# Expert outputs of a mixture-of-experts stage: row sums gathered and added on VectorE and stored plainly, instead of an adding scatter; experts taken in an order that alternates their groups

## The reference

```python
p_group = jax.nn.softmax(hf @ w_group, axis=-1)
g_sel = jnp.argmax(p_group, axis=-1)          # one group for each token
le = logits_e[token, g_sel]                   # the 8 experts of that group
top_v, top_i = lax.top_k(le, 2)               # two experts, both of the group
gate = g_w[:, None] * jax.nn.softmax(top_v, axis=-1)
...
y = (jax.nn.silu(xb @ w_gate[e]) * (xb @ w_up[e])) @ w_down[e]
out = segment_sum(y * row_w, row_tok)         # x + out is the result
```

## Time and profile before

| what | value |
|---|---|
| median of 3 runs | 1223.68 us (1217.13 to 1223.85) |
| the profiled execution's own time | 1217.27 us |
| its span, first to last instruction | 1215.5 us |
| PE busy | 1111.2 us, 91% of the span |
| DVE, ACT, POOL busy | 438.8, 328.7, 168.2 us |
| moved by DMA | 297.60 MB in 84831 packets |

### The profile page before, as it was taken

How to read it: one execution, slowest core, us unless ns; L and a number is a source line. 1 busy time by engine, 2 the same in 40 slices (tenths; PEclk the granted TensorE clock), 3 DMA queues, 4 the chain that set the end, 5 groups by cost and what they waited for, 6 DMA issues and landing times.

```text
span 1215.5 us, 26688 instructions
## 1 busy us (share of the span) xinstructions
PE 1111.2 (91%) x11558; PEld 802.1 (66%) x11558; DVE 438.8 (36%) x803; ACT 328.7 (27%) x642; POOL 168.2 (14%) x149
## 2 busy tenths in 40 slices
PE   3998899999997987999949999999999998989995
PEld 3998899976664534889846666666666655655563
DVE  3424564348674532335452212222222212212121
ACT  4422232146574542222211111111111111111111
POOL 0000110299200000000010111111111111111110
PEclk9999898999898997999959999999999999999998
DMA  5326786000105441945588999999999999999983
GB/s 192 120 71 182 213 252 203 1 12 2 36 1 173 139 174 70 297 173 228 193 348 332 380 367 380 371 385 367 373 376 375 372 368 379 382 380 372 373 325 57
DMA packets 84831, 297.60 MB, mean 245 GB/s; under 512 B 11393, under 2 KB 42817, under 8 KB 59095
## 3 DMA queue, kind: packets, MB, share of 16 engines
q1 hardware_dynamic: 77543, 274.48, 61.1%
q0 software_dynamic: 7168, 21.37, 7.7%
HBM read 272.98 MB, written 43.66 MB: 260 GB/s over the span
## 4 chain that ended last, share of the span: by engine, by line
PE 73%; DMA 15%; DVE 4%; SPq 3%; ACT 3%; issue 2%; POOL 0%; ACTq 0%; POOLq 0%; DVEq 0%
DMA w_ring<-in_w_up 11%; PE bank L1987 9%; PE bank L2227 8%; PE bank L2371 8%; PE bank L2375 7%; PE bank L2379 6%; PE bank L2039 4%; PE bank L2405 4%; PE bank L2409 4%; PE bank L2204 3%; PE bank L2168 3%; PE bank L2413 3%; PE bank L2077 3%; PE bank L2350 2%; DMA out_k_all<-kn 2%
## 5 line engine op out<-in xcount | busy, mean ns | idle before, releaser
L2371 PE MATMUL bank<-w_ring,xeT 128*32 128x256 f32 x1536 | 347.1, 383 | 0.0
L2375 PE MATMUL bank<-w_ring,xeT 128*32 128x512 f32 x1536 | 269.7, 600 | 14.7 <-DMA w_ring<-in_w_up 14.0
L2371 PEld LDWEIGHTS bank<-w_ring,xeT 128*32 128x32 f32 x1536 | 166.9, 111 | 55.3 <-issue 2.0
L2405 PE MATMUL bank<-w_ring,hT 128*32 128x256 f32 x768 | 171.7, 380 | 0.0
L2379 PE MATMUL bank<-w_ring,xeT 128*32 128x256 f32 x1536 | 157.9, 382 | 0.0
L1873 DVE SCALAR_TENSOR_TENSOR hid<-sgl,gtab,bank 96x256 f32<-96x256 f32 x32 | 21.9, 685 | 356.3 <-ACT sgl L1433 356.3
L2409 PE MATMUL bank<-w_ring,hT 128*32 128x512 f32 x768 | 133.2, 595 | 1.6 <-ACT hT L1439 1.6
L1987 PE MATMUL bank<-w_hi,xh 128*128 128x256 f32 (+1 forms) x432 | 125.4, 290 | 2.5 <-DVE xl L1495 2.4
L1987 PE MATMUL bank<-w_lo,xh 128*128 128x256 f32 (+1 forms) x432 | 122.3, 283 | 0.0
L1987 PE MATMUL bank<-w_hi,xl 128*128 128x256 f32 (+1 forms) x432 | 122.2, 283 | 0.0
L1622 DVE TENSOR_TENSOR_SCAN keep<-keep,unseen 128x1024 f32<-128x1024 f32 (+7 forms) x64 | 87.8, 1404 | 69.1 <-ACT keep L1233 69.1
(11 more groups left out here) (259 smaller groups left out, 1645.1 us busy)
## 6 DMA issues: line engine op xcount, KB each, us to landing
w_ring<-in_w_gate SPq DMA_DIRECT2D x64, 1024.0 KB, 32.3
w_ring<-in_w_up SPq DMA_DIRECT2D x64, 1024.0 KB, 30.6
w_ring<-in_w_down SPq DMA_DIRECT2D x64, 1024.0 KB, 32.1
w_raw<-in_w_in SPq DMA_DIRECT2D x8, 1024.0 KB, 6.9
k_scr<-in_cache_k SPq DMA_DIRECT2D x32, 256.0 KB, 3.6
v_scr<-in_cache_v SPq DMA_DIRECT2D x32, 256.0 KB, 3.3
pgk<-k_scr SPq DMA_DIRECT2D x32, 256.0 KB, 4.1
pgv<-v_scr SPq DMA_DIRECT2D x4, 1024.0 KB, 6.0
```

Source lines behind the costliest of these rows:

```text
L2371: return pe.matmul(up_right_ps(i, g), xeT[i][:, k, rows_of(g)], w[1][:, k, FA:F], start=first and g != 1, stop=ends, skip_group_check=True)
L2375: pe.matmul(gate_ps(i)[rows_of(g), :], xeT[i][:, k, rows_of(g)], w[0][:, k, :], start=first, stop=ends, skip_group_check=True)
L2405: return pe.matmul(y_right_ps(g), hT[:, ft, rows_of(g)], w[:, ft, DA:D], start=first and g != 1, stop=ends, skip_group_check=True)
```

## The change

- `scatter` is a plain indirect store: no addition in the DMA, empty slots left out (bounds T - 1, as in `gather`). `y_all` and `n_scr` lose their spare rows, and the two transfers that filled these with zeros (L928, L929) go.
- A new indirect DMA, `gather_sums(b)`, gathers the rows' sums so far from `y_all` into `yo[b % 2]`, before block b's product is added to it. GpSimd sets both `yo` to zero at first, since empty slots stay unwritten.
- `add_rows` on VectorE takes the place of `left_rows` on ScalarE and `right_rows` on VectorE: five additions, PSUM plus `yo` into `yo` (96 x 512, 96 x 256, three of 32 x 256), after a wait for the gathered sums. TensorE's `down_product` waits for it alone.
- On GpSimd the order for each block is now: gather_sums(b + 1) once scatter b - 1 has landed, scatter(b), gather(b + 4). Gather and scatter no longer end in a wait of their own (`moved` is gone).
- Block b is expert 8 (b mod 4) + b // 4 instead of expert b, so that two neighbouring blocks belong to different groups and share no token; gather_sums(b + 1) can then be issued before scatter(b).
- Two small tables (`cmp`, `past`) move to another place in SBUF, because `yo` is in use earlier.

```diff
+    def expert_of(b):
+
+        return EPG * (b % NGRP) + b // NGRP
...
-            sp.wait_ge(s_zr, 2)
-            sp.dma_start(n_scr[T:NY, :], zrow[:, :]).then_inc(s_yst, 16)
-            sp.dma_start(y_all[T:NY, :], zrow[:, :]).then_inc(s_yst, 16)
...
-            pool.memset(zrow[:, :], 0.0).then_inc(s_zr, 1)
-            pool.wait_ge(s_zr, 2)
+            for i in range(2):
+                pool.memset(yo[i][:, :], 0.0).then_inc(s_zr, 1)
...
-            def scatter(b):
-
-                pool.wait_ge(s_ya, b + 1)
-                pool.wait_ge(s_yd, b + 1)
+            def gather_sums(b):
+
+                i = b % 2
+                pool.wait_ge(s_sc, 16 * (b - 1)) if b >= 2 else pool.wait_ge(s_zr, 3)
                 if b >= NE:
                     pool.wait_ge(s_sx2, b - NE + 1)
+                pool.indirect_dma_start(out=yo[i][:, :], out_offset=None, in_=y_all,
+                                        in_offset=bass.IndirectOffsetOnAxis(ap=rows_named(b, sidx), axis=0),
+                                        bounds_check=T - 1, oob_is_err=False).then_inc(s_ga[i], 16)
+
+            def scatter(b):
+
+                pool.wait_ge(s_yd, b + 1)
                 pool.indirect_dma_start(out=y_all,
                                         out_offset=bass.IndirectOffsetOnAxis(ap=rows_named(b, sidx), axis=0),
-                                        in_=yo[b % 2][:, :], in_offset=None, compute_op=ALU.add,
-                                        bounds_check=NY - 1).then_inc(s_sc, 16)
-
-            def moved(b):
-
-                if b < NE - 3 or b >= NE:
-                    pool.wait_ge(s_gl[(b + 3) % 2], 16 * ((b + 3) // 2 + 1))
-                pool.wait_ge(s_sc, 16 * (b + 1))
+                                        in_=yo[b % 2][:, :], in_offset=None,
+                                        bounds_check=T - 1, oob_is_err=False).then_inc(s_sc, 16)
...
-            for b in range(3):
+            for b in range(2):
                 gather(b)
+            gather_sums(0)
+            for b in range(2, 4):
+                gather(b)
 
             for b in range(NE - 1):
-                if b + 3 < NE:
-                    gather(b + 3)
+                gather_sums(b + 1)
                 scatter(b)
-                moved(b)
+                if b + 4 < NE:
+                    gather(b + 4)
...
-            def left_rows(b, i):
-
-                act.wait_ge(s_dp, 8 * b + 8)
-
-                since(act, s_sc, 16 * b - 16)
-                act.activation(yo[i][:, 0:512], y_left_ps, ACT.Copy)
-                for g in range(2):
-                    last = act.activation(yo[i][rows_of(g), DA:D], y_right_ps(g), ACT.Copy)
-                last.then_inc(s_ya, 1)
...
-            def right_rows(b, i):
+            def add_rows(b, i):
                 dve.wait_ge(s_dp, 8 * b + 8)
-
-                since(dve, s_sc, 16 * b - 16)
-                dve.tensor_copy(yo[i][:, 512:DA], y_mid_ps)
-                dve.tensor_copy(yo[i][rows_of(2), DA:D], y_right_ps(2)).then_inc(s_yd, 1)
+                dve.wait_ge(s_ga[i], 16 * (b // 2 + 1) if type(b) is int else 8 * (b - i) + 16)
+                dve.tensor_tensor(yo[i][:, 0:512], y_left_ps, yo[i][:, 0:512], ALU.add)
+                dve.tensor_tensor(yo[i][:, 512:DA], y_mid_ps, yo[i][:, 512:DA], ALU.add)
+                for g in range(LANES):
+                    rows = rows_of(g)
+                    last = dve.tensor_tensor(yo[i][rows, DA:D], y_right_ps(g), yo[i][rows, DA:D], ALU.add)
+                last.then_inc(s_yd, 1)
...
             def down_product(b, i):
                 w = weights_of(b, i, 2)
                 pe.wait_ge(s_hl, b + 1)
-                since(pe, s_ya, b)
                 since(pe, s_yd, b)
```

More of the change, by code:

```diff
@@ L62 @@
 OVMAX = -(-T // CAP) - 1
-NY = T + CAP
 NCONST = 3
@@ L524, in hybrid_step @@
     s_tbl = sem("router_tables_ready")
-    s_zr = sem("zero_rows_ready")
+    s_zr = sem("zero_logits_and_rows_ready")
     s_ssq2 = sem("sumsq2_ready")
@@ L547, in hybrid_step @@
     s_gc = sem("block_gates_ready")
-    s_sx2 = sem("scatter_rows_named")
+    s_sx2 = sem("sum_rows_named")
+    s_ga = [sem(f"sums_gathered{i}") for i in range(2)]
     s_gl = [sem(f"gathered{i}") for i in range(2)]
@@ L558, in hybrid_step @@
     s_dp = sem("down_product")
-    s_ya = sem("left_rows_copied")
-    s_yd = sem("right_rows_copied")
+    s_yd = sem("rows_added")
     s_sc = sem("block_scattered")
@@ L672, in hybrid_step, with column_of @@
     OVER = ((6, 7, 8), (2, 3, 5))
+    def expert_of(b):
+        return EPG * (b % NGRP) + b // NGRP
+    def column_of(b):
+        return expert_of(b) if b < NE else b
     assert not {parts.index((NE - 1, j)) % NWS for j in range(3)} & set(OVER[0])
@@ L948, in _ @@
                 load_part(q)
-            sp.wait_ge(s_yst, 16 * (NT + 2))
+            sp.wait_ge(s_yst, 16 * NT)
             sp.wait_ge(s_lgp, NT)
@@ L1079, in rows_named @@
             def rows_named(b, further):
-                return (tab[:, b:b + 1] if b < NE else further[b % 2][:, 0:1]).bitcast(U32)
+                return (tab[:, column_of(b):column_of(b) + 1] if b < NE else further[b % 2][:, 0:1]).bitcast(U32)
             def gather(b):
@@ L1128, in _ @@
                     pool.wait_ge(s_gl[(NE + i) % 2], 16 * ((NE + i) // 2 + 1))
-                pool.wait_ge(s_sc, 16 * NE)
                 for o in range(OVB):
                     with pool.If(n_over > o):
+                        pool.wait_ge(s_sc, 16 * (NE + o))
+                        gather_sums(NE + o)
                         gather(NE + o + 3)
                         scatter(NE + o)
-                        moved(NE + o)
+                        pool.wait_ge(s_gl[(NE + o + 3) % 2], 16 * ((NE + o + 3) // 2 + 1))
+                        pool.wait_ge(s_sc, 16 * (NE + o + 1))
         @block.scalar
@@ L1459, in block_act @@
                 block_left(b + 2, i)
-                left_rows(b, i)
             def last_act(b):
@@ L1465, in last_act @@
                     silu(b + 1, 1)
-                left_rows(b, b % 2)
             def resume_act():
@@ L1858, in hidden @@
                 if type(b) is int:
-                    gates = gtab[:, b:b + 1]
+                    gates = gtab[:, column_of(b):column_of(b) + 1]
                 else:
@@ L1898, in block_dve @@
                 block_right(b + 2, i)
-                right_rows(b, i)
+                add_rows(b, i)
             def last_dve(b):
@@ L1903, in last_dve @@
                     hidden(b + 1, 1)
-                right_rows(b, b % 2)
+                add_rows(b, b % 2)
             def resume_dve():
@@ L2463, in _ @@
             blocks(pe, first_pe, block_pe, last_pe, resume_pe, further_pe)
-_OUTS = {"y_all": (NY, D), "k_all": (T, AW), "v_all": (T, AW), "pool_p": (HIST, PW), "pool_s": (DB, HIST, PW)}
+_OUTS = {"y_all": (T, D), "k_all": (T, AW), "v_all": (T, AW), "pool_p": (HIST, PW), "pool_s": (DB, HIST, PW)}
 _LAYERED = ("cache_k", "cache_v", "state_pool", "w_in", "w_pool", "w_out", "w_group", "w_expert", "w_gate", "w_up",
```

15 lines of the change are left out of this document (7 added, 8 removed).

## The result

The changed kernel takes 1248.90 us (median of four runs, 1246.64 to 1256.80), the one before 1220.95 beside it: 28 us more, a ratio of 1.024, 95% interval 1.020 to 1.029. Forecast were 1235, +11 on the kernel before. The sign and the bound (the weight stream pays) hold; the size is two and a half times the forecast. The profile is of the slowest of the four runs, 1256.8 us with a span of 1255.0, so some 8 us of it are no part of what is to be explained; the profile of before lies 3.7 us under its own median.

What follows compares the result with a forecast made beforehand. The prediction took the weight stream to set the end, although TensorE is busy nearly all the time. Stream +11.5 us and tail -0.6 gave about +11 on the 1223.7 us median, 1235, range 1208 to 1252.

Steps and rivals of the forecast that it cites:

- The adding scatter goes: -1.93: Weight stream, each block: removing the 96-row adding scatter gives back 1.93 us.
- The gather of the sums comes: Weight stream, each block: the new gather costs 1.70 us, priced like the existing gather of block rows.
- The sentence on the ports: DMA into SBUF: partition decides which of 16 ports is used; 128-partition transfers keep each engine on its own port.
- The plain scatter comes: Weight stream, each block: a plain scatter costs only its bytes, 67 rows, 0.64 us.
- theory 2: Follow-up theory on GpSimd's transfers: the DMA engine with most rows sets the price; spreading saves 0.8 us a block.
- The sum for a block: Weight stream: -1.93 + 1.70 + 0.64 = +0.41 us a block, +11.5 us over 28 blocks.
- VectorE and the new wait: VectorE's additions, 2.37 us a block, stay hidden in steady state; the gathered sums arrive with 12 us to spare.
- Rival C: GpSimd's new wait: landings taking twice as long make the sums late; 1250 us and more, chance 0.03.
- The tail, -0.6 us: Kernel's end: +0.4 and +1.0 from later additions, -0.2 and about -1.8 from the plain last scatter.
- A: Weight stream: packets alone count, the gather of sums does not slow weights; faster, 1209 us, chance 0.18.
- B: Weight stream: plain scatter rows cost as adding ones, 1.35 us; +1.12 us a block, 1254 us, chance 0.12.
- D: Weight stream: gather of sums at about 1.3 us, no change, 1224 us, chance 0.10.

Runs made afterwards that it cites:

- e1: Changed kernel without the gathers of sums, VectorE adding onto whatever lies in yo: 1203.18 us, ratio 0.988 to the kernel before.
- e6: Kernel before, its adding scatter leaving out empty slots and each expert's rows spread over the slots: 1201.55 us, ratio 0.985.
- e7: Kernel before, its adding scatter leaving out empty slots and its gather of rows over 128 slots: 1202.43 us, ratio 0.987.
- e2: Changed kernel with the sums gathered from n_scr instead of y_all: 1253.23 us, ratio 1.029 to the kernel before.
- e8: Changed kernel, but gather b+4 waits until scatter b has landed: 1254.61 us, ratio 1.031 to the kernel before.
- e5: Changed kernel with each expert's rows spread over the slots: 1225.46 us, ratio 1.006 to the kernel before.
- e9: Changed kernel with both gathers, block rows and sums, over 128 slots: 1216.14 us, ratio 0.999 to the kernel before.
- e4: Kernel before, with its adding scatter leaving out empty slots and nothing else changed: 1219.61 us, ratio 1.002.

## Why the prediction was right and wrong, step by step

- **The bound.** Right. The weight stream sets the end in both kernels, and whatever frees it (e1, e6, e7) stops at TensorE's floor, at 1201.6 to 1203.2 us; the forecast's floor was 17.9 us under the profile of before, 1199.4.
- **"The adding scatter goes: -1.93."** Right as a window, but it hid a rule. With 96 rows in 96 slots bytes and fullest engine give the same, so the scatters of the kernel before could not tell them apart.
- **"The gather of the sums comes", 1.70 us.** Right in kind, a little low: 1.86 by e1, the upper end of the forecast's 1.58 to 1.9. The forecast saw that its two prices explain 95% of the loss; the rest, 0.19 us, belonged to the gather. e2 shows that it is priced like any gather. The sentence on the ports pointed the right way: it spoke against the change, and the 128-slot form takes about 0.6 us off such a gather.
- **"The plain scatter comes", 0.64 us. This is the step that failed**, the term mis-sized: it measured 0.9 to 1.05 us by e1 and 1.15 in e8's windows. "So a plain store costs its bytes: 67 rows" counted the mean engine. The packets themselves are as cheap as said: in e1 q0 has 9.0% of 460 us of 16 engines, 41.4 us, of which 26 gathers at 0.91 take 23.7; 0.66 us are left for each scatter, 0.157 a row and engine. Six rows of these, as theory 2 puts on the fullest engine, are 0.94 us, an estimate that fits what was measured. The earlier trace rows could not warn of it: those stores had full tiles.
- **The sum for a block**: +0.85 instead of +0.41, over 28 blocks +24 instead of +11.5. The scatter's 0.3 to 0.4 us are the larger part of the miss, the sums' 0.16 the smaller.
- **The first wait** came "some blocks earlier": at 13 instead of 20. **"The waits in all 11 us longer"**: 20 us.
- **VectorE and the new wait.** Right: 2.38 us for the additions, hidden; the sums land 9.0 us after issue, the median; no addition waits for them. Rival C did not happen.
- **The tail, -0.6 us: wrong, it is +5.** Products 30 and 31 end 9.61 us apart instead of 7.45, and the span ends 13.8 us after product 31 instead of 10.6. The windows from 1228 us of the kernel after show the first part (PE, PEld, DVE, ACT, POOL busy, then the granted clock):

```profile
1228.00:1232.00 4.00, 3.96 (x54) 2.39 (x45) 2.25 (x4) 0.01 (x1) 0.00 (x0) 1.00 0.23 61
1232.00:1234.00 2.00, 0.00 (x0) 0.01 (x1) 1.88 (x5) 0.48 (x1) 0.00 (x0) 1.00 0.00 0
1234.00:1238.00 4.00, 3.98 (x32) 2.30 (x36) 0.00 (x0) 0.00 (x0) 0.94 (x1) 0.57 0.24 68
1238.00:1242.00 4.00, 3.09 (x48) 1.79 (x39) 0.81 (x2) 0.00 (x0) 0.00 (x0) 1.00 0.02 4
```

TensorE stands for 2.06 us while add_rows(30) runs (before, 1.56 us for the copy of hT), 0.5 us longer, where 0.4 was forecast. Then the granted clock is 0.57 for 4 us: most of them at 1.2 GHz, which costs 4 x 0.43 = 1.7 us. After the 1.56 us the clock stayed at 1.00. But the pause alone does not decide it. e1, e5 and e9 have the same fall (0.60 or 0.61 in the 4 us behind the pause), while e2 and e8 pause for as long, 2.07 us in e2, and stay at full clock; their products 30 and 31 end 7.93 us apart. e2, the first 4 us behind its pause:

```profile
1231.30:1235.30 4.00, 4.00 (x61) 2.73 (x57) 0.00 (x0) 0.00 (x0) 0.94 (x1) 1.00 0.24 68
```

So 1.7 of the 5 us come in some kernels and not in others that differ only elsewhere, and why is open. The second part: the last rows come 1.0 us later, as forecast, but from the start of the last scatter's instruction to the end there are 10.6 us, against 8.4 before. The last scatter itself did become shorter, as forecast: it lands 3.6 us after its start instead of 5.5. What grew is what follows. SyncE's last wait, after the landing, in the kernel after and in the one before (us in total, times, longest):

```profile
SPq L723 <- PEq L723: 6.8, 1, 6.8
...
SPq L716 <- PEq L716: 2.6, 1, 2.6
```

It is 4.2 us in e1, which has the plain scatter but no gather of sums. From the start of the last scatter to the end there are 10.6 us in e5 and e9 too, and 8.0 in e1. So 4.2 us more stand behind the last landing, and part of it came with the third indirect transfer of each block. Why is open.

- **The rivals.** A was wrong, and for a reason worth keeping: the bytes of a transfer are not its price. Nor did the rule that an adding row counts twice decide it: the adding rows are as dear as it says (0.33 us against 0.157), and the gain from plain ones, 1.93 to about 1.0 us, is still seven tenths of what the bytes give; and the gather of the sums slows the weights, which A leaves out. B came out in size, 1254 against 1248.9, by luck: its 1.35 us are too high by as much as the forecast's 0.64 was too low, and its tail of -0.6 made up for it. Nor is its reason the one: single rows are cheap, 0.157 us of an engine. D did not happen.

+24 us from the stream and +5 in the tail are 29; measured are 28. In the two profiled executions, which lie 7.9 us over and 3.7 under their medians, the spans differ by 39.5 us: 4.0 before product 0, 25.3 up to product 28, 4.8 up to product 30 and 5.4 behind it.

## What to carry to other kernels

Do not price an indirect transfer beside a saturated stream by its bytes alone; the engine with most rows gave the better estimate here. Spread the rows over the slots, and only then skip the empties (together -18 us here, skipping alone 0). Give a gather into SBUF the same number of partitions as the loads it runs beside, even if the extra slots are empty (-0.6 us a gather here). And read the price of a transfer over a long stretch that ends before the stream does, in every kernel that is compared: windows at the start of this stage read 0.99 us where the mean was 1.68, and a stretch that ran past the stream's end made one gather 0.3 us too cheap.

## What the runs showed of the hardware

- Leaving out 29 of 96 rows of a scatter changed the time by nothing (e4, 1.002, 0.999 to 1.004); the same rows spread over the slots were worth 18 us more (e6).
- 32 empty slots added to a gather made it cheaper: 1.63 to 0.83 us beside the weights in one window, 1.80 to 1.00 on the mean of 24 and 25 (e4, e7).
- A skipped slot of an indirect transfer still had a packet: 111 or 112 packets with some 67 or with 96 rows in 96 slots (e4, before), 144 with 128 slots (e7).
- A row of an adding scatter took 0.33 us of an engine (before), a plain one 0.157 (e1).
- A pause of TensorE of 2.06 us, with work on both sides, was followed by a granted clock of 0.57 over 4 us (after), and one of 2.07 us by none (e2, clock 1.00).
